# A two-layer trunk kernel: the ring slots of the second mixer turned, its cache, state and projections loaded ahead of the pairs of rows, and another load order ahead of the second experts

## The reference

```python
def odd_mixer(h, p, rope, ctx):
    z = h @ p['w_in']                                   # 1024 -> 384 + 256 + 32
    cq, ckv, kpe = jnp.split(z, (C_Q_LORA, C_Q_LORA + C_KV_LORA), axis=-1)
    q = (rms_norm(cq, p['g_qa']) @ p['w_uq'])           # 384 -> 16 heads x 96
    ckv = rms_norm(ckv, p['g_kva'])
    k, v = mla_expand(ckv, kpe, p['w_ukv'], p['g_k'])   # 256 -> 16 heads x (64 + 64)
    kc, vc = mla_expand(ctx[0], ctx[1], p['w_ukv'], p['g_k'])   # the cache, sample only
    return dense_attention(q, concat(kc, k), concat(vc, v)) @ p['w_o']
```

## Time and profile before

| | |
|---|---|
| median of 3 runs | 993.45 us (993.09 to 996.7) |
| profiled execution | 995.68 us |
| its span, first to last instruction | 993.9 us |
| mean granted TensorE clock | 0.974 of 2.4 GHz |
| TensorE busy (matmul) | 894.8 us, 90% of the span |
| VectorE, ScalarE, GpSimd busy | 407.2, 239.6, 120.1 us |
| DMA | 318.85 MB, mean 321 GB/s |

### The profile page before, as it was taken

How to read it: one execution, slowest core, us unless ns; L and a number is a source line. 1 busy time by engine, 2 the same in 40 slices (tenths; PEclk the granted TensorE clock), 3 DMA queues, 4 the chain that set the end, 5 groups by cost and what they waited for, 6 DMA issues and landing times.

```text
span 993.9 us, 14410 instructions
## 1 busy us (share of the span) xinstructions
PE 894.8 (90%) x5457; PEld 499.1 (50%) x5457; DVE 407.2 (41%) x1184; ACT 239.6 (24%) x604; POOL 120.1 (12%) x131
## 2 busy tenths in 40 slices
PE   4999889999999999887899998998989999997880
PEld 2345436547555565444356564555655555544440
DVE  2102476346622442211363666564764225321214
ACT  3111144111111111111344455333211111111111
POOL 1000000100222222211100000001001222222120
PEclk9999999999999999999999999999999999998995
DMA  9989799739899999998760029606699999999965
GB/s 374 399 333 404 289 421 416 257 137 363 350 417 417 410 417 418 418 418 315 278 233 6 1 94 377 260 1 189 217 420 400 417 419 408 417 416 419 413 276 197
DMA packets 61685, 318.85 MB, mean 321 GB/s; under 512 B 12598, under 2 KB 13878, under 8 KB 31528
## 3 DMA queue, kind: packets, MB, share of 16 engines
q1 hardware_dynamic: 46144, 285.84, 71.4%
q0 software_dynamic: 13328, 25.02, 7.4%
q10 hardware_dynamic: 2144, 7.06, 1.8%
HBM read 312.72 MB, written 26.49 MB: 341 GB/s over the span
## 4 chain that ended last, share of the span: by engine, by line
PE 65%; DMA 20%; DVE 9%; ACT 2%; issue 2%; SPq 1%; DVEq 0%; POOLq 0%; ACTq 0%
PE psum L916 16%; DMA ring<-in_l_w 15%; PE psum L929 9%; PE psum L1135 7%; PE psum L1247 3%; PE psum L852 3%; PE psum L865 3%; PE psum L896 2%; PE psum L1256 2%; PE psum L696 2%; PE psum L1339 1%; DMA ring<-in_ada_first 1%; PE psum L1361 1%; PE psum L922 1%; PE psum L1288 1%
## 5 line engine op out<-in xcount | busy, mean ns | idle before, releaser
L916 PE MATMUL psum<-ring,scratch 128*64 128x256 f32 x1744 | 210.2, 393 | 25.8 <-DMA ring<-in_l_w 25.7
L916 PEld LDWEIGHTS psum<-ring,scratch 128*64 128x64 f32 x1744 | 135.6, 141 | 85.0 <-issue 37.6
L2254 DVE TENSOR_TENSOR scratch<-scratch,psum 64x256 f32<-64x256 f32 x64 | 27.2, 425 | 291.7 <-ACT scratch L1531 285.9
L929 PE MATMUL psum<-ring,scratch 128*64 128x512 f32 x464 | 112.8, 607 | 1.9 <-ACT scratch L1579 1.0
L2721 POOL DMA_INDIRECT expert_rows<-scratch,slot_rows x64 | 63.5, 991 | 343.1 <-ACT scratch L1545 343.1
L1531 ACT ACTIVATE scratch<-psum 64x256 f32<-64x256 f32 x64 | 24.0, 375 | 260.2 <-PE psum L916 257.0
L1135 PE MATMUL psum<-ring,scratch 128*128 128x512 f32 x192 | 73.5, 540 | 1.5 <-DVE scratch L1862 1.5
L1545 ACT COPY scratch<-psum 128x512 f32<-128x512 f32 x64 | 37.5, 586 | 133.6 <-PE psum L929 133.6
L1135 PEld LDWEIGHTS psum<-ring,scratch 128*128 128x128 f32 x192 | 36.0, 190 | 36.6 <-issue 35.5
L929 PEld LDWEIGHTS psum<-ring,scratch 128*64 128x64 f32 x464 | 29.6, 137 | 42.1 <-issue 37.9
L2236 DVE COPY scratch<-psum 128x512 f32<-128x512 f32 x64 | 41.5, 687 | 7.9 <-PE psum L878 6.8
(11 more groups left out here) (383 smaller groups left out, 1215.0 us busy)
## 6 DMA issues: line engine op xcount, KB each, us to landing
ring<-in_l_w SPq DMA_DIRECT2D x108, 1024.0 KB
ring<-in_l_w_rows SPq DMA_DIRECT2D x56, 1024.0 KB
ring<-in_l_w_ada SPq DMA_DIRECT2D x40, 1024.0 KB, 5.4
ring<-in_ada_first SPq DMA_DIRECT2D x8, 1024.0 KB
ring<-in_l_w_o SPq DMA_DIRECT2D x8, 1024.0 KB
ring<-in_l_w_in SPq DMA_DIRECT2D x4, 1024.0 KB
gate_rows<-gate_rows_hbm POOLq DMA_DIRECT2D x8, 512.0 KB, 7.9
scale_shift<-gate_rows_hbm POOLq DMA_DIRECT2D x8, 512.0 KB, 10.7
```

The lines of the kernel that those rows point to most:

```text
L916: last = nc.tensor.matmul(ps[64 * n:64 * n + 64, 2 + par, 0:DE], mine[:, k, :], part(w, k * DE, DE), start=k == 0, stop=k == KD - 1)
L929: last = nc.tensor.matmul(ps[64 * n:64 * n + 64, 5 + par, :], hhT[:, par, k, :], part(w2, k * D + n * 512, 512), start=k == 0, stop=k == 1)
```

## The change

Units of the second mixer are renumbered: the up projection for keys and values comes first (slots 4 and 5), then the input weights (6 to 8), then the query weights (9 to 11). Queries, heads and probabilities move by two slots with them. The cache gets a place in slot 3. SyncE's order becomes: cache, state, up projection, input weights, pairs, query weights. In `load_experts(1)` the 12 ring loads come in the order (0,0), (0,1), (0,2), (1,0), (1,1), (2,1), (2,2), (1,2), (2,0), (3,0), (3,1), (3,2), with the waits moved to the loads whose slots they guard.

```diff
-U_WIN1 = 136
-U_UQ = 139
-U_UKV = 142
+U_UKV = 136
+U_WIN1 = 138
+U_UQ = 141
...
 def used(unit):
-    return unit + 1 if unit < U_MOE[0] else unit + 1 - MOE_UNITS
+    if unit < U_MOE[0]:
+        return unit + 1
+    if unit < U_WIN1 or U_UQ <= unit < U_WO[1]:
+        return U_WO[1] - MOE_UNITS
+    return unit + 1 - MOE_UNITS - (U_WIN1 - U_UKV if unit < U_UQ else 0)
...
-        qT1 = view(ring[:, 4:7, :].rearrange("p s n -> p (s n)"), 0, NT, C_HEADS, P)
-        catT1 = view(ring[:, 7:9, :].rearrange("p s n -> p (s n)"), 0, KD, NT, P)
-        pT1 = view(ring[:, 9, :], 0, 2, 768)
+        qT1 = view(ring[:, 6:9, :].rearrange("p s n -> p (s n)"), 0, NT, C_HEADS, P)
+        catT1 = view(ring[:, 9:11, :].rearrange("p s n -> p (s n)"), 0, KD, NT, P)
+        pT1 = view(ring[:, 11, :], 0, 2, 768)
+        cachew = view(ring[:, 3, :], 0, KV_LORA + ROPE)
...
-                if last >= U_MOE[0] and last < U_WIN1:
+                if last >= U_MOE[0] and last < U_UKV:
...
                 if l:
-                    first = first[6:8] + first[0:3] + first[5:6] + first[8:] + first[3:5]
+                    first = first[0:5] + first[7:9] + first[5:7] + first[9:]
                 for u, n in first:
-                    if (u, n) == ((2, 0) if l else (2, 2)):
+                    if (u, n) == ((0, 0) if l else (2, 2)):
...
-                    if l and (u, n) in ((2, 0), (2, 1)):
+                    if l and (u, n) in ((0, 0), (0, 1)):
                         sp.wait_ge(S["ada_used"], KD)
-                    if l and u == 0:
-                        sp.wait_ge(S["scores_in_psum"], len(MIX0) + (len(ATT1) if n else 4))
-                    if l and (u, n) == (1, 2):
+                    if l and (u, n) == (0, 2):
+                        sp.wait_ge(S["scores_in_psum"], len(MIX0) + 4)
+                    if l and (u, n) in ((1, 0), (1, 1)):
+                        sp.wait_ge(S["scores_in_psum"], len(MIX0) + len(ATT1))
+                    if l and (u, n) == (2, 1):
                         sp.wait_ge(S["att_in_psum"], len(MIX0) + len(ATT1))
-                    if l and (u, n) in ((1, 0), (1, 1)):
+                    if l and (u, n) in ((1, 2), (2, 0)):
                         sp.wait_ge(S["units_used"], used(U_WO[1] + 3))
...
             load_experts(0)
+            sp.dma_start(cachew[:, 0:KV_LORA], A["cache_l1_ckv"].rearrange("a s d -> (a s) d")).then_inc(S["cache_in"], 16)
+            sp.dma_start(cachew[:, KV_LORA:], A["cache_l1_kpe"].rearrange("a s d -> (a s) d")).then_inc(S["cache_in"], 16)
+            load_state(0)
             for k in range(2):
                 load(U_UKV + k, SLOT, A["l1_w_ukv"][k * P:(k + 1) * P, :])
-            sp.wait_ge(S["up_done"], NE)
-            sp.dma_start(ckvw[:, 3, 0:KV_LORA], A["cache_l1_ckv"].rearrange("a s d -> (a s) d")).then_inc(S["cache_in"], 16)
-            sp.dma_start(ckvw[:, 3, KV_LORA:], A["cache_l1_kpe"].rearrange("a s d -> (a s) d")).then_inc(S["cache_in"], 16)
-            load_state(0)
-            load_pairs(0)
             for n, (k0, k1) in enumerate(((0, 3), (3, 6), (6, 8))):
                 load(U_WIN1 + n, (k1 - k0) * ODD_IN,
                      A["l1_w_in"][k0 * P:k1 * P, :].rearrange("(k p) n -> p k n", p=P), k1 - k0)
 
+            load_pairs(0)
             sp.wait_ge(S["pair_rows2"], 32)
```

More of the change, by code:

```diff
@@ L1226, in transpose_c @@
                 for k in range(2):
-                    last = nc.tensor.transpose(ps[:, kv_bank, k * P:(k + 1) * P], ckvw[:, t, k * P:(k + 1) * P], ident)
+                    src = ckvw[:, t, :] if t < 3 else cachew
+                    last = nc.tensor.transpose(ps[:, kv_bank, k * P:(k + 1) * P], src[:, k * P:(k + 1) * P], ident)
                 last.then_inc(S["cT_in_psum"], 1)
@@ L1752, in _ @@
             act.wait_ge(S["cache_in"], 32)
-            link(nc.scalar.activation(junk[:, 0:ROPE], ckvw[:, 3, KV_LORA:], ACT.Square,
+            link(nc.scalar.activation(junk[:, 0:ROPE], cachew[:, KV_LORA:], ACT.Square,
                                       scale=QK ** -0.5, accum_out=s1[:, 9:10]))
@@ L2624, in _ @@
             dve.wait_ge(S["cache_in"], 32)
-            link(V.tensor_tensor(kr[:, 3, :], ckvw[:, 3, KV_LORA:], gkr, ALU.mult))
+            link(V.tensor_tensor(kr[:, 3, :], cachew[:, KV_LORA:], gkr, ALU.mult))
             unit(0)
```

## The result

The changed kernel takes 1000.75 us (median of 20 runs, 997.19 to 1004.71). The kernel before, run beside it on the same chip, takes 996.85 us (20 runs, 991.75 to 1001.35). The ratio is 1.0038, 95% interval 1.0021 to 1.0055: 3.8 us slower, between 2.1 and 5.5. I had forecast +1.7 us. The predicted 995.2 us and its range to 998.0 miss the measured time for two reasons: the cost was over twice as large, and the 993.45 us from which I counted was the median of three runs at the low end of what 20 runs show. The second says nothing about the change, so what follows goes by differences. One execution of the kernel of e1 took 1535 us at a granted clock of 0.566, and its ratio leaves that slow run out.

A forecast was written before the change was run, and what follows sets the result against it. Between expert stages the chain through TensorE was taken to bound, at 498.5 the row write, pairs and norm; inside them, DMA. Terms 0 + 0 + 1.7 + 0 + 0 gave +1.7 us on 993.45, forecast 995.2, 80% range 989.2 to 998.0.

The forecast's parts named there:

- third rival: First transition: late engines' input-weight backlog past 488.2 thins the write and delays the pairs; +5.2 us, 998.7; chance 0.11.
- (a): First transition, TensorE: the 2.85 us cache wait goes, worth nothing; expansion and fillers end earlier, about 494.1.
- (b): Last row write and pairs: late engines' backlog ends at 488.8, pairs start within 0.5 us of before; 0, bounds -4.1, +2.6.
- (c): TensorE before tile 0's transposes: idle some 4.4 us, lower clock slows transposes and first projection; +1.7 us, bounds 0 and 2.6.
- (d): Query weights still wait for the pairs; first used after 540, so up to 2.6 us later costs nothing.
- The gap I had bounded at 2.6 us: DMA loss after the load at 708.44, ahead of the second experts; 1.2 us slack absorbs it; cost 0, bounds 0 and 1.5.
- The first rival: First transition: engines empty in time, write lands after 2.7 us, pairs and transposes 4.1 us earlier; 989.4; chance 0.25.
- Signs: Early issues by 452 and 466, no cache wait, 4 us idle before tile 0's transposes, granted clock near 0.5 there.
- within 0.5%: Whole kernel: the change stays within 5 us of no change, what a measurement can tell; chance 0.82.

The follow-up runs named there:

- e1: Changed kernel with the three input-weight loads put back behind the pairs; ratio to the kernel before 0.9988 (0.9967-1.0009).
- e3: Changed kernel with the query weights also issued ahead of the pairs (5.11 MB ahead instead of 2.75); ratio to the kernel before 1.0111.
- e7: Changed kernel with one input-weight load (1.03 MB) ahead of the pairs and two behind; ratio to the kernel before 1.0020 (0.9996-1.0044).
- e12: Changed kernel with its input-weight loads held until expert 31's up projection is done, still ahead of the pairs; ratio to the kernel before 1.0052.
- e2: Changed kernel with only the load order ahead of the second experts put back; ratio to the kernel before 1.0045 (1.0026-1.0064).
- e6: Kernel before with only the new load order ahead of the second experts; ratio to the kernel before 0.9987 (0.9965-1.0010).
- e5: Changed kernel with input weights behind the pairs and the old load order ahead of the second experts; ratio to the kernel before 1.0000.
- e9: Changed kernel with input weights behind the pairs and the up projection for keys and values held until expert 31's up projection is done; ratio 0.9975 (0.9953-0.9997).
- e8: Changed kernel with input weights behind the pairs, and cache, state and key/value projection held until expert 31's up projection is done; ratio 1.0024 (0.9996-1.0051).
- e4: Changed kernel with 12 instead of 9 filling matmuls before the transposes of tile 0; ratio to the kernel before 1.0040 (1.0018-1.0062).

## Why the prediction was wrong, point by point

**The mechanism was named, as the third rival, and given too small a chance.** "The input weights hold up the pairs" had 0.11, and e1, e3, e7 and e12 show it by removal, by dose and by delay. Its place, the pairs on SyncE's queue, was right. Its total, +5.2, was above the measured 3.8, and its terms were others: of its three prices, +2.0 for the write, +0.6 for the pairs, +2.6 for the clock, the profile shows -0.3, +5.3 and +0.8, with -1.9 ahead of the write that it did not have. That the totals lie near each other is chance.

**(a)** The cache wait went and was worth nothing, as said. "Expansion and filling ... end at 479.2 + 7.0 + 7.9, about 494.1" was wrong: I didn't ask what would be late next for TensorE. My own sum in (b) had the answer: with 4.87 MB ahead of its end, the up projection was on a late engine until 479.8 at the least (468.1 and 11.7 us at 417 GB/s), and later with GpSimd's share. It landed at 480.1 and 483.2, TensorE waited for it 5.37 us at 480.30, and the fillers ended at 498.0. The kernel paid nothing for it, since the row chain was later still.

**(b) is the step that failed.** "The pairs, whose first bytes could not move before about 488 anyway ... start within half a microsecond of where they did. I take 0 for this term." By the yardstick the first pair was ready 3.1 us later than before (49.85 against 46.77 us from expert 28's start). Two parts of the step were wrong.

The smaller is the comparison. I set the end of the backlog, 488.8, beside the first byte of the pairs and not beside their landing. Two loads for tile 0 are 1.05 MB; on a late engine they start at 488.8 and need 2.5 us more at 417 GB/s, 491.3 in all. Before, the pair had landed at 490.84 although it was issued at 486.23, because at 486 to 488 the DMA share was down to 0.35. So my own sum gave +0.5 and not 0, and its 488.8 was already past the 488.2 from which I had said that the third rival decides.

The larger is the end of the backlog itself. The last input load landed at 490.3 and the pair of tile 0 at 492.8, just the 2.5 us of 1.05 MB at 417 GB/s. This profile starts its stretch 1.05 us earlier than that of before (443.02 against 444.07), so 490.3 stands for 491.4 there: 2.6 us later than 488.8, though expert 31's weights had landed 0.7 earlier. From that landing to the end of the backlog the slowest engine took 23.9 us (466.39 to 490.3), where I had counted 20.7 for its share of 7.6 MB and GpSimd's 1 MB. Both parts together, 0.5 and 2.6, are the 3.1.

Since the last write was issued 1.9 us earlier by the yardstick and the backlog does not move with it, that head start was lost in the queue too.

Why the slowest engine took 3.2 us longer than my sum stays open. In e1 the up projection is the last thing in the backlog, and its chain says

```profile
461.71 23.18 DMA ring<-in_l_w_ukv
484.94 5.42 PE psum L1254 x12
```

From expert 31's landing at 470.77 to 484.94, 14.2 us, the slowest engine had its sixteenth of 4.87 MB to move (1.05 + 0.15 + 1.57 + 2.10): 344 GB/s if all sixteen went at its pace and GpSimd moved nothing, or, with all of GpSimd's 1 MB, the 14.1 us that I would have counted. The same bytes took 16.8 us in the kernel after (466.39 to 483.2). Behind them the landings at 483.2, 486.2, 488.6 and 490.3 make 344, 430 and 405 GB/s. So 2.7 of the 3.2 us were lost ahead of 483.2.

The Trainium skill, "DMA: Bandwidth & Descriptors", section "Queues, rings and completion order", has an engine go round its queues by packets, with one ring per queue. The rows after agree: the write, on GpSimd's queue, is thinned by the stream beside it (6.50 us, where e1 with less beside it has 2.53), and the pairs, on the ring that also holds the input weights, wait until those have landed (9.87 us against 4.57). I had applied the rule to the write alone.

**(c)** +1.7 forecast, +1.64 measured, and the agreement is luck, since it came on another row: TensorE idled 2.54 us instead of 4.4, the transposes kept 2.4 GHz (1.09 us) and the first projection did not (8.69). Half of it, 0.86 us, came back by tile 2, most of that from the 0.68 us wait of the earlier trace rows that I had called no cover; it fell to 0.16.

**(d)** No cost of the query weights shows, and none of the second experts' order (e2, e6). The gap I had bounded at 2.6 us is there (two issues in 5.48 us from 713.28), and the queue still ran thin ahead of expert 0's slots, more than before (184 and 201 GB/s at 754 to 758, against 320 and 274), so there was slack to take it in.

**The first rival** (0.25), engines empty in time, is not this change but the one that e1, e5 and e9 made of it. Its price between write and transposes was right: forecast 4.1, measured 4.3. Its end result was not, as 2 us were lost ahead of the write, and in e1 the fillers end at 498.08, just when the rows are ready: TensorE's own chain is the bound again.

**Signs.** Of the signs that I had named, the cache came without a wait. The issue times did not come true: the first half of the up projection went out at 457.03 and not by 452, the last input load at 469.2 and not by 466, as SyncE needed 7.20 us for the three state loads. The idle time before the transposes was 2.54 us and not 4, and their clock was full.

**Chances.** 0.82 stood on "within 0.5%", and the ratio is there. The sign of the forecast was right; its size was not, and for the reason in (b).

## What stays open

Expert 31's weights, issued before anything that was moved, landed 24.4 us after their issue in the kernel before, 25.4 to 25.7 in e1, e5 and e7, 24.6 to 24.9 in e8 to e12, and 23.4 to 23.8 in the kernels with the input weights issued from 461 on (after, e2, e3, e4). The 24.9 of e12 beside the 25.4 of e1 shows that half a microsecond is chance. The first difference could be traffic behind them on the late engines. The last goes the other way, more traffic and an earlier landing, and e12 did not decide between cause and chance. It is worth 1 to 2 us, as much as the gain that is left. Open too is why the backlog of the slowest engine took 3.2 us longer than my sum, and whether 1 MB ahead of the pairs has a cost that many runs would show (e7, 1.0020, between 0.9996 and 1.0044).

## What to carry to other kernels

Ahead of a transfer that everything waits for, count what its own queue still holds on the slowest DMA engine, at that engine's pace, and compare landing with landing, not with the first byte. A prefetch belongs behind such a transfer unless it has landed before that is issued: in the profiles here 1 MB lengthened the write, and 2.75 MB the pairs. When a load is made early, the next late one takes its place, so ask for it by name, and look at the small gain that can be had (cache and state ahead, everything else behind) before moving all of it.

## What the runs showed of the hardware that I had not expected

**SyncE is slowed by its own backlog.** The three state loads took 7.20 us to issue at 449.78, up to 4.58 for one of them, against 1.68 in the earlier trace rows and 1.4 in e8. A small load behind a long stream is late before it is issued.

**The end of a long stream is spread widely.** The engines were busy to 0.47 and 0.40 on average at 480 to 484 while the landing took until 492.8, and a landing time is one of the slowest engine.

**The clock is not a function of the last waits.** The first projection ran in part at the lower clock after waits of 0.23 and 1.60 us in e9 (granted 0.50 at 499 to 501), and at the full clock after 0.26 and 1.59 in e6 and after no wait and 1.59 in e1. All three had done the same fillers and transposes just before:

```profile
495.91 1.09 PE L746 MATMUL psum<-constants,scratch 128*128 128x128 f32 x8 [0.23 <-DVE scratch L1890]
498.60 8.70 PE L1204 MATMUL psum<-ring,scratch 128*128 128x384 f32 x24 [1.60 <-ACT scratch L1473]
```

```profile
500.60 7.05 PE L1203 MATMUL psum<-ring,scratch 128*128 128x384 f32 x24 [1.59 <-ACT scratch L1472]
```

```profile
499.90 1.09 PE L739 MATMUL psum<-constants,scratch 128*128 128x128 f32 x8 [0.26 <-DVE scratch L1882]
502.59 7.05 PE L1197 MATMUL psum<-ring,scratch 128*128 128x384 f32 x24 [1.59 <-ACT scratch L1465]
```

The order is e9, e1, e6. In the kernel before, the 32 matmuls of an up projection took 5.36 us after a wait of 1.85 (at 402.81) and 3.67 after one of 1.95 (at 451.78). That is 1.6 us either way in one profile, and a reason to judge terms of this size by many runs.
